# Eleven groups of three small products of ones between the first products of the dense part

## The chip, the cores and the metric

The kernel runs on all 8 cores of one Trainium2 chip, every core with the same program on one sequence of the batch of 8. A core has TensorE (PE; its weight loads are shown apart, as PEld), VectorE (DVE), ScalarE (ACT), GpSimd (POOL) and SyncE (SP), which meet by semaphores. The metric is the device time in microseconds of the slowest core, as the median of several runs.

## The reference

A decoder trunk of two layers on x of shape (8, 2048, 1024) in float32, with a conditioning vector c per sequence. Each layer has three parts, and each part is: RMSNorm, shift and scale from c, a function, a gate from c, and a residual add.

```python
for l in range(DEPTH):
    mod = c_act @ w_mod[l] + b_mod[l]
    ...
    h, gate = modulate(x, norm_g[l, 0], mod_f1)
    x = x + 0.5 * gate * swiglu(h, w_ffn_in[l, 0], w_ffn_out[l, 0])
    h, gate = modulate(x, norm_g[l, 1], mod_mx)
    ...
    x = x + gate * y
    h, gate = modulate(x, norm_g[l, 2], mod_f2)
    x = x + 0.5 * gate * swiglu(h, w_ffn_in[l, 1], w_ffn_out[l, 1])
return rmsnorm(x, final_g)
```

`swiglu` multiplies by two matrices of 1024 x 2816 and one of 2816 x 1024. The mixer `y` is a spatial gating and a short convolution between two projections in the first layer, and a causal pooling with small products in the second. Nearly all arithmetic lies in the matrix products. Those of the feed-forward parts and of the mixer's input are built in the kernel as seven block products in the place of eight, by sums of blocks of the weights and of the activations that DVE makes.

## The kernel before, in words

A core keeps its 2048 x 1024 residual stream in on-chip memory (X, four tiles of 512 tokens) and goes through ten phases: for each of five sub-layers (two feed-forward parts, the mixer, two feed-forward parts, with the pooling mixer worked in beside them) two passes of 1024 tokens. In a phase, weights come as pieces of 128 x 2048 floats by DMA from POOL's queue into six slots (SLOTS), normed activations stand in H, and products of 128 x 128 weights with 512 columns go into the eight PSUM banks (ps). ACT and DVE take them from there into ACTB, from which the second matrix is applied; DVE adds the result to X. `gu_segments` (line 1031) issues the first products of a feed-forward part and its inner `prod` four products into one bank. These products, with an index of `Sd.fill_to` (line 1723) or above, are called the dense part here.

Before the dense part stands a start of some 55 us: X and the first rows of the modulation weights arrive, ACT squares X, PE sums the squares by products with a block of ones (ONES, 128 x 128 in bf16), DVE and ACT build H. So that PE isn't idle, up to 150 (WARM, line 25) filler products of ones with squares (SQ) are put in, into bank 5:

```python
for n in range(WARM):
    op = add("pe", I("matmul", PS[5][:], ONES[:], SQ[:, n % NSQ, :], start=True, stop=True, skip_group_check=True),
             reads=[("SQ", n % NSQ), "ONES"], writes=[("ps", 5)], cost=0.0)
    op.issue, op.filler = c_pe(TT), 1
```

All instructions are entered into one list with what they read and write. `Sched.add` gives each a start time by a cost model, `Sched.relist` (line 178) goes through the list again and moves instructions of DVE, ACT and PE to where the model has them ready, most urgent first. It runs twice (line 1862). Fillers are taken only until the 21st product of the dense part has started (line 225). `Sched.emit` (line 281) then sorts by start time and writes out each engine's instructions in that order, with semaphore waits where another engine's work is needed:

```python
order = sorted((o for o in ops if o.filler < 2), key=lambda o: (o.start, o.idx))
...
for o in order:
    o.pos = len(by_eng[o.eng])
    by_eng[o.eng].append(o)
```

So a start time that is set after the last `relist` decides the place in an engine's queue, and nothing else. All instructions are issued by one helper, `I` (line 479), so the profile has all of them on line 480, and the names of what they write and read tell them apart: ps<-SQ,ONES are sums of squares and fillers, ps<-H,SLOTS and ps<-ACTB,SLOTS the dense part, ps<-ACTB the 128-column products of the spatial gating (`z_part`, line 1431).

Of the kernel before, what the change touches and what calls it, by code (L numbers as in the profile page):

```python
# [23 lines left out]
R_AT = 21  # L24
WARM = 150
PASSES = 2
SLG = (5, 6, 6, 7, 7, 7)


# [54 lines left out]
class Sched:  # L84
# [23 lines left out]
    def add(self, eng, fn, reads=(), writes=(), cost=0.1, dma=None, nbytes=0, after=0.0):  # L108

        ops = self.ops  # L110
        idx = len(ops)
        reads = list(reads)
        writes = list(writes)
        for k in list(reads):
            if isinstance(k, tuple) and k[0] == "ps":
                reads.remove(k)
                writes.append(k)
        deps = set()
        for k in reads:
            w = self.lastw.get(k)  # L120
            if w is not None:
                deps.add(w)
        for k in writes:
            w = self.lastw.get(k)
            if w is not None:
                deps.add(w)
            deps.update(self.readers.get(k, ()))
        choices = eng if isinstance(eng, list) else [(eng, fn, cost)]
        best = None
        for e, f, c in choices:  # L130
            ready = after
            for d in deps:
                o = ops[d]
                if o.eng == e and o.semkey is None and e == "pe":
                    t = o.end
                elif o.semkey is not None:
                    t = o.end
                else:
                    t = o.end + self.LAT[o.eng]
                if t > ready:  # L140
                    ready = t
            t = self.tl[e].find(ready, c)
            if best is None or t + c < best[0] - 1e-9:
                best = (t + c, t, e, f, c)
        _, t, e, f, c = best
        self.tl[e].put(t, c)
        op = Op()
        op.idx = idx
        op.eng = e
        op.fn = f  # L150
        op.deps = deps
        op.semkey = dma
        op.issue = c
        op.nbytes = nbytes
        op.bw = self.BW
        op.after = 0.0
        op.then = None
        op.gate = set()
        op.filler = 0
        op.start = t  # L160
        op.end = t + c
        if dma is not None:
            w = nbytes / self.BW
            s = self.wire.find(op.end + 1.5, w)
            self.wire.put(s, w)
            op.end = s + w + 2.0
        op.signal = False
        op.seq = 0
        op.dma_target = 0
        ops.append(op)  # L170
        for k in writes:
            self.lastw[k] = idx
            self.readers[k] = []
        for k in reads:
            self.readers.setdefault(k, []).append(idx)
        return op
# [302 lines left out]
def I(name, *a, **k):  # L479
    return lambda E: getattr(E, name)(*a, **k)  # L480
# [4 lines left out]
def build_nc():  # L485
# [37 lines left out]
    ONES = sb("ONES", [128, 128], BF16)  # L523
# [10 lines left out]
    PS = [nc.alloc_psum_tensor("ps%d" % b, [128, TT], F32) for b in range(8)]  # L534

    Sd = Sched()
    add = Sd.add
# [67 lines left out]
    def Xk(c, t):  # L605
        return ("X", c, t)
# [101 lines left out]
    def load_next(slot, after=()):  # L708
        if stream_at[0] >= len(stream):
            return  # L710
        pc = stream[stream_at[0]]
        stream_at[0] += 1
        pc.slot = slot
        pc.loaded = True
        if pc.kept is None:
            op = add("pool", I("dma_start", out=SL[:, slot, 0:pc.n], in_=pc.src, max_dma_last_dim=8192),
                     reads=list(after), writes=[("SL", slot, q) for q in range(7)], cost=0.7, dma=("SL", slot), nbytes=128 * 4 * pc.n)
        else:
            add("sp", I("dma_start", out=SL[:, slot, 1536:3584], in_=sums_d[pc.kept]), reads=[("SUMS", pc.kept)],
                writes=[("SL", slot, q) for q in range(3, 7)], cost=0.06, dma=("SS", slot), nbytes=128 * 4096)  # L720
            op = add("pool", I("dma_start", out=SL[:, slot, 0:1536], in_=pc.src[:, 0:1536], max_dma_last_dim=6144),
                     reads=list(after), writes=[("SL", slot, q) for q in range(3)], cost=0.7, dma=("SL", slot), nbytes=128 * 6144)
        pc.ready = op.end
# [951 lines left out]
    for t in range(2):  # L1675
        add("sp", I("dma_start", out=X[:, t, :, :], in_=xT[t].rearrange("p (c k) -> p c k", k=TT)),
            writes=[Xk(c, t) for c in range(NC)], cost=0.06, dma=("X", t), nbytes=128 * 16384)
# [15 lines left out]
# [3 lines that stand above are left out]
# [18 lines left out]
    fin["n", 0, 0] = True  # L1714
    for s, k in zip(range(NSLOT), SLG):
        load_next(s, [("MOD", 0, order0[k])])
# [3 lines left out]

    Sd.BW = Sched.BW

    Sd.fill_to = len(Sd.ops)


# [45 lines left out]
    for k, ph in enumerate(PHASES):  # L1771
# [6 lines left out]
        if sub[0] == "F":  # L1778
            l, i = sub[1], sub[2]
            s = 2 * i  # L1780
            for g in range(len(GROUPS)):
# [39 lines left out]
                if pm is not None:  # L1821
                    if pm == 0:
                        add("dve", I("memset", STAT[:, 0, 15:16], 0.0), reads=[("MOD", 0, q) for q in range(144)],
                            writes=["PMFREE", "CB"] + [("WM", x) for x in range(NWM)] + [("STG", x) for x in range(4)], cost=0.05)
# [36 lines left out]
    add("sp", None, reads=[("OUT", t, c) for t in range(4) for c in ((1, 3, 5, 7) if t < 3 else range(NC))], cost=0.01)  # L1861
    for _ in range(PASSES):
        Sd.relist(("dve", "act", "pe"))
    with nc.Block() as block:
        Sd.emit(nc, block)
    nc._sched = Sd
# [33 lines left out]
```

## Time and profile before

| | us |
|---|---|
| median of 3 runs | 1942.34 (1941.77 to 1942.77) |
| profiled execution, its own time | 1939.81 |
| its span, slowest core (core 0) | 1938.2 |
| spans of the other cores | 1906.8 to 1934.4 |
| PE busy in the span of core 0 | 1893.0 |
| DVE busy | 1719.3 |
| ACT busy | 1056.7 |
| POOL busy | 183.0 |

The span is the time from a core's first to its last instruction. Busy time of an engine is the time in which it had an instruction at work; products are pipelined, so one takes longer than the time from it to the next. The granted clock is the share of full speed (2.4 GHz) that the chip's throttle gave TensorE; 0.50 is the lower of its two levels, 1.2 GHz. A windows view has one row for a stretch: its length, then for PE, PEld, DVE, ACT and POOL the busy time and in brackets the number of instructions, then the mean granted clock, the share of the 16 DMA engines that was busy, and GB/s. In a row of instructions in order of time stand the start, the time from there to the end of the last one, the engine, the operation with what it writes and reads, the shape, and how many such instructions follow one another.

### The profile page before, as it was taken

How to read it: one execution, taken by the hardware profiler on the slowest of the kernel's cores; microseconds unless marked ns; L12 is line 12 of the kernel's file. 1: busy time of each engine (PE TensorE's matmuls, PEld its weight loads, DVE VectorE, ACT ScalarE, POOL GpSimd, SP SyncE). 2: the span in 40 equal slices, each digit the busy share in tenths (PEclk: the TensorE clock that was granted, in tenths of full speed). 3: DMA queues.
4: the chain of work that ended last, by engine and by line, in shares of the span. 5: the costliest groups of instructions: out<-in, count | busy, mean ns of one | idle time of the engine just before them, and what ended most of it. 6: DMA issues, size and time to landing. Idle time of an engine off the chain costs nothing.

```text
span 1938.2 us, 25442 instructions; the slowest of 8 cores (1906.8 to 1938.2 us)
## 1 busy us (share of the span) xinstructions
PE 1893.0 (98%) x8633; PEld 849.7 (44%) x8633; DVE 1719.3 (89%) x3326; ACT 1056.7 (55%) x1782; POOL 183.0 (9%) x349
## 2 busy tenths in 40 slices
PE   5999999999999999999999999999999999999997
PEld 2444444444444444444444444444444444444443
DVE  5886899989898999999999999998998899898865
ACT  4443755455757664565456545554556655574343
POOL 0000000000303000000000000000000000000000
PEclk6888899999999999999999999999999999999999
DMA  9867648755676668876877677745454545545852
GB/s 290 158 142 164 130 88 185 148 102 114 127 150 169 141 130 175 168 148 140 175 160 155 128 169 166 156 80 99 74 95 69 88 77 90 85 70 88 173 90 92
DMA packets 69390, 254.22 MB, mean 131 GB/s; under 512 B 7824, under 2 KB 7952, under 8 KB 69008
## 3 DMA queue, kind: packets, MB, share of 16 engines
q0 software_dynamic: 42192, 152.85, 47.4%
q1 hardware_dynamic: 26784, 98.96, 15.8%
q8 instruction: 73, 1.20, 0.2%
q10 hardware_dynamic: 288, 0.79, 0.1%
q14 instruction: 53, 0.43, 0.1%
HBM read 393.86 MB, written 11.53 MB: 209 GB/s over the span
## 4 chain that ended last, share of the span: by engine, by line
PE 93%; DMA 3%; ACT 2%; DVE 1%; SPq 0%; issue 0%; POOL 0%
PE ps L480 93%; DMA X<-xT 1%; DMA SLOTS<-win 1%; DMA WMOD<-wmod 1%; ACT SQ L480 1%; ACT TP L480 1%; DVE ACTB L480 0%; SPq L480 0%; ACT H L480 0%; ACT ps L480 0%; DVE X L480 0%; DVE TP L480 0%; DVE ps L480 0%; ACT L480 0%; ACT ACTB L480 0%
## 5 line engine op out<-in xcount | busy, mean ns | idle before, releaser
L480 PE MATMUL ps<-H,SLOTS 128*128 128x512 f16 x5376 | 1204.9, 384 | 8.1 <-ACT ps L480 3.4
L480 PEld LDWEIGHTS ps<-H,SLOTS 128*128 128x128 f16 x5376 | 527.7, 99 | 662.6 <-issue 90.0
L480 ACT ACTIVATE ps<-ps 128x512 f32<-128x512 f32 x716 | 416.3, 582 | 611.9 <-PE ps L480 601.5
L480 PE MATMUL ps<-ACTB,SLOTS 128*128 128x512 f16 x2780 | 623.1, 382 | 0.0
L480 PEld LDWEIGHTS ps<-ACTB,SLOTS 128*128 128x128 f16 x2780 | 273.9, 99 | 334.0 <-issue 26.4
L480 DVE TENSOR_TENSOR SLOTS<-SLOTS 128x512 f16<-128x512 f16 x1036 | 408.9, 417 | 10.6 <-DMA SLOTS<-win 6.1
L480 DVE SCALAR_TENSOR_TENSOR X<-ps,GH,X 128x512 f32<-128x512 f32 x424 | 307.8, 745 | 45.2 <-PE ps L480 38.6
L480 ACT ACTIVATE TP<-ps 128x512 f32<-128x512 f32 x408 | 241.6, 594 | 94.1 <-PE ps L480 89.7
L480 DVE TENSOR_TENSOR ACTB<-TP,ps 128x512 f16<-128x512 f32 x352 | 236.8, 682 | 34.4 <-PE ps L480 24.2
L480 POOL DMA_DIRECT2D SLOTS<-win x176 | 93.1, 530 | 1057.9 <-PE ps L480 993.1
L480 DVE TENSOR_TENSOR TP<-ps,TP 128x512 f32<-128x512 f32 x192 | 131.8, 687 | 55.6 <-ACT ps L480 54.4
L480 ACT ACTIVATE SQ<-X 128x512 bf16<-128x512 f32 x224 | 131.3, 623 | 85.1 <-DVE X L480 50.5
L480 DVE SCALAR_TENSOR_TENSOR WMOD<-WMOD,CB 128x1024 f32<-128x1024 f32 x130 | 157.8, 1216 | 3.0 <-DMA WMOD<-wmod 3.0
L480 DVE TENSOR_TENSOR ps<-ps,TP 128x512 f32<-128x512 f32 x192 | 133.4, 695 | 15.6 <-PE ps L480 12.4
L480 DVE TENSOR_TENSOR TP<-X,RS 128x512 f32<-128x512 f32 x192 | 127.8, 683 | 6.5 <-ACT ACTB L480 4.0
L480 DVE TENSOR_TENSOR ACTB<-ACTB 128x1024 f16<-128x1024 f16 (+1 forms) x188 | 103.9, 564 | 0.9
L480 ACT ACTIVATE H<-TP,MODT,AS 128x512 f16<-128x512 f32 x105 | 81.2, 806 | 31.9 <-DVE TP L480 31.6
L480 POOL DMA_DIRECT2D SLOTS<-wout x88 | 46.4, 528 | 496.8 <-PE ps L480 496.8
L480 PE MATMUL ps<-SQ,ONES 128*128 128x512 bf16 x173 | 58.1, 435 | 25.5 <-ACT SQ L480 23.4
L480 DVE TENSOR_TENSOR H<-H 128x1024 f16<-128x1024 f16 (+1 forms) x88 | 53.9, 634 | 1.7 <-ACT H L480 1.6
L480 ACT ACTIVATE PMH<-TP,MODT,AS 128x512 f16<-128x512 f32 x52 | 41.4, 806 | 11.8 <-DVE TP L480 11.6
L480 PEld LDWEIGHTS ps<-SQ,ONES 128*128 128x128 bf16 x173 | 18.3, 108 | 54.6 <-issue 41.2
(79 smaller groups left out, 548.5 us busy)
## 6 DMA issues: line engine op xcount, KB each, us to landing
SLOTS<-win POOLq DMA_DIRECT2D x176, 512.0 KB, 5.9
WMOD<-wmod SPq DMA_DIRECT2D x131, 512.0 KB, 5.3
SLOTS<-wout POOLq DMA_DIRECT2D x88, 512.0 KB, 5.4
SLOTS<-wab POOLq DMA_DIRECT2D x22, 512.0 KB, 6.4
outT<-X SPq DMA_DIRECT2D x14, 512.0 KB, 4.1
ACTB<-wmod SPq DMA_DIRECT2D x13, 512.0 KB, 24.9
X<-xT SPq DMA_DIRECT2D x2, 2048.0 KB, 20.7
X<-xT SPq DMA_DIRECT2D x8, 512.0 KB, 5.2
```

The lines of the kernel that those rows point to most:

```text
L480: return lambda E: getattr(E, name)(*a, **k)
```

## The change

Before the dense part is entered, 33 products are added to the list: ONES times ONES, 128 columns, into bank 7, in groups of three. After the last `relist` the products of the dense part are sorted by start time, and each group gets a start just behind that of the dense product whose number stands in SOFT, so that the groups stand behind the products 0, 1, 2, 4, 6, 8, 12, 15, 18, 22 and 27.

```diff
--- before.py
+++ after.py
@@ -24,6 +24,8 @@
 R_AT = 21
 WARM = 150
 PASSES = 2
+
+SOFT = (0, 1, 2, 4, 6, 8, 12, 15, 18, 22, 27)
 SLG = (5, 6, 6, 7, 7, 7)
 
 
@@ -1720,6 +1722,13 @@
 
     Sd.BW = Sched.BW
 
+    soft = []
+    for at in SOFT:
+        for n in range(3):
+            op = add("pe", I("matmul", PS[7][:, 0:128], ONES[:], ONES[:], start=True, stop=True, skip_group_check=True), reads=["ONES"],
+                     writes=[("ps", 7)], cost=0.0)
+            op.issue = 0.0
+            soft.append((at, op))
     Sd.fill_to = len(Sd.ops)
 
 
@@ -1861,6 +1870,9 @@
     add("sp", None, reads=[("OUT", t, c) for t in range(4) for c in ((1, 3, 5, 7) if t < 3 else range(NC))], cost=0.01)
     for _ in range(PASSES):
         Sd.relist(("dve", "act", "pe"))
+    dense = sorted((o for o in Sd.ops if o.eng == "pe" and o.idx >= Sd.fill_to), key=lambda o: o.start)
+    for n, (at, op) in enumerate(soft):
+        op.start = dense[at].start + 0.001 * (n + 1)
     with nc.Block() as block:
         Sd.emit(nc, block)
     nc._sched = Sd
```

PE's queue at the end of the start, before (H and SLOTS: activations and weights of the dense part; SQ, ONES: fillers):

```order
L480 MATMUL ps<-SQ,ONES 128x512 x19
L480 MATMUL ps<-H,SLOTS 128x512 x8
L480 MATMUL ps<-SQ,ONES 128x512 x2
L480 MATMUL ps<-H,SLOTS 128x512 x316
L480 MATMUL ps<-ACTB,SLOTS 128x512 x7
```

The dense part began there with 8 products in a row, 2 fillers, and 316 in a row.

The same place now, from the same fillers on:

```order
L482 MATMUL ps<-SQ,ONES 128x512 x19
L482 MATMUL ps<-H,SLOTS 128x512
L482 MATMUL ps<-ONES 128x128 x3
L482 MATMUL ps<-H,SLOTS 128x512
L482 MATMUL ps<-ONES 128x128 x3
L482 MATMUL ps<-H,SLOTS 128x512
```

Of the 8 products each of the first three is followed by a group of three.

And further down, where the last groups stand:

```order
L482 MATMUL ps<-H,SLOTS 128x512 x3
L482 MATMUL ps<-ONES 128x128 x3
L482 MATMUL ps<-H,SLOTS 128x512 x4
L482 MATMUL ps<-ONES 128x128 x3
L482 MATMUL ps<-H,SLOTS 128x512 x5
L482 MATMUL ps<-ONES 128x128 x3
L482 MATMUL ps<-H,SLOTS 128x512 x296
L482 MATMUL ps<-ACTB,SLOTS 128x512 x7
```

The last group stands behind the 28th product of the dense part; 296 products in a row follow it where 316 did.

On DVE, ACT, POOL and SP the order of instructions is the same as before.

## Rows read from the trace of the kernel before

**Rows 1.** Spans of all cores, us, with the mean granted clock.
```profile
core 0: 1938.2 us, clock 0.973
core 1: 1934.4 us, clock 0.979
...
core 3: 1907.0 us, clock 0.994
...
core 5: 1907.6 us, clock 0.988
core 6: 1911.1 us, clock 0.989
core 7: 1906.8 us, clock 0.994
```

**Rows 2.** The page, core 0: PE's busy time; shares of the chain.
```profile
PE 1893.0 (98%) x8633; PEld 849.7 (44%) x8633; DVE 1719.3 (89%) x3326; ACT 1056.7 (55%) x1782; POOL 183.0 (9%) x349
PE 93%; DMA 3%; ACT 2%; DVE 1%; SPq 0%; issue 0%; POOL 0%
```

**Rows 3.** Windows of core 0: length, busy us (count) by engine, clock, DMA.
```profile
core 0: us, PE busy (x) PEld busy (x) DVE busy (x) ACT busy (x) POOL busy (x), PEclk, DMA share, GB/s
54.00:58.00 4.00, 4.00 (x20) 1.86 (x19) 3.12 (x9) 2.47 (x5) 0.00 (x0) 1.00 1.01 220
60.00:62.00 2.00, 2.00 (x9) 0.75 (x8) 2.00 (x6) 1.67 (x4) 0.00 (x0) 0.87 1.06 168
62.00:219.00 157.00, 157.00 (x599) 64.87 (x598) 120.61 (x237) 66.36 (x114) 11.09 (x21) 0.81 0.71 155
219.00:221.00 2.00, 2.00 (x9) 0.84 (x8) 2.00 (x5) 1.60 (x4) 0.00 (x0) 0.88 0.65 129
221.00:300.00 79.00, 79.00 (x367) 35.82 (x366) 76.24 (x147) 52.96 (x94) 6.87 (x13) 1.00 0.52 94
300.00:1900.00 1600.00, 1591.03 (x7400) 718.65 (x7399) 1463.64 (x2806) 891.34 (x1507) 157.75 (x302) 1.00 0.63 126
```

**Rows 4.** Windows of core 1.
```profile
60.00:62.00 2.00, 2.00 (x10) 0.75 (x9) 1.92 (x6) 1.05 (x2) 0.00 (x0) 0.89 1.08 178
62.00:219.00 157.00, 157.00 (x600) 64.95 (x599) 120.76 (x235) 67.09 (x115) 11.07 (x21) 0.81 0.73 156
```

**Rows 5.** Windows of core 3, of the same die as core 0.
```profile
60.00:62.00 2.00, 1.97 (x10) 0.77 (x9) 2.00 (x6) 1.05 (x2) 0.00 (x0) 1.00 0.94 166
62.00:219.00 157.00, 156.90 (x727) 70.77 (x726) 143.70 (x287) 85.41 (x146) 13.73 (x26) 1.00 0.81 169
```

**Rows 6.** PE of core 0 in order of time, 48 to 76 us.
```profile
48.65 7.02 PE L480 MATMUL ps<-SQ,ONES 128*128 128x512 bf16 x19
55.51 1.89 PE L480 MATMUL ps<-H,SLOTS 128*128 128x512 f16 x8
57.24 0.59 PE L480 MATMUL ps<-SQ,ONES 128*128 128x512 bf16 x2
57.67 18.73 PE L480 MATMUL ps<-H,SLOTS 128*128 128x512 f16 x73
```

**Rows 7.** PE of core 2 in order of time, 590.5 to 591.5 us.
```profile
590.55 0.39 PE L480 MATMUL ps<-ACTB 128*128 128x128 f16 x4
590.78 0.38 PE L480 MATMUL ps<-H,SLOTS 128*128 128x512 f16 x1
590.99 0.39 PE L480 MATMUL ps<-ACTB 128*128 128x128 f16 x4
591.22 1.03 PE L480 MATMUL ps<-H,SLOTS 128*128 128x512 f16 x4
```

**Rows 8.** Groups of PE by form: busy us, mean ns of one, idle before.
```profile
L480 PE MATMUL ps<-ACTB 128*128 128x128 f16 x64 | 5.2, 219 | 0.9 <-ACT TP L480 0.8
```

## The prediction

> **What bounds the kernel now.** Start with the spans and granted clocks of all cores [rows 1]. Six cores end between 1906.8 and 1911.1 us; core 0 takes 1938.2 and core 1 takes 1934.4, with a mean granted clock of 0.973 and 0.979 where the six have 0.988 or more. The metric is the slowest core, so the time is core 0's, some 27 us behind the slowest core of the rest. All cores run the same program on equally large inputs, so the two differ in the clock and not in work.
>
> The page and the chain that ended last say what bounds a core: PE is busy for 98% of the span and makes 93% of the chain [rows 2]. Whatever slows a TensorE product, or is put between two of them, goes to the end nearly one to one.
>
> The windows of core 0 tell when its clock is low [rows 3]. From 54 to 58 us it is at 1.00, the upper of the two levels (2.4 GHz). Between 60 and 62 the mean is 0.87, from 62 to 219 it is 0.81, between 219 and 221 it is 0.88, and then 1.00 until 1900. So 0.81, a value between the levels 0.50 and 1.00, begins at 62 - 2 x 0.13 / 0.19 = 60.6 us and ends at 219 + 2 x 0.12 / 0.19 = 220.3 us: one stretch of about 160 us. On core 1 the same sum gives 60.8 for the start, and it has the same 0.81 stretch [rows 4]. Core 3, of the same die, has the same kind of work at those times and stays at 1.00 [rows 5].
>
> What PE did before the fall stands in its instructions in order of time [rows 6]. Until 55.51 us core 0 ran products on ones and squares. Then come 8 products on real data, 2 on ones, and from 57.67 an unbroken run of products on real data, each 512 columns at 2.4 GHz. The clock falls 5.1 us after the first of them and 2.9 us after the start of the run.
>
> Price of the stretch: between 62 and 219 us core 0 ran 599 products and core 3 ran 727 [rows 3, 5]. One at full clock takes 157 / 727 = 0.216 us, so core 0 lost 128 x 0.216 = 27.6 us there, and 27.6 x 159.7 / 157 = 28.1 us in the whole stretch. Without it core 0 would end at 1938.2 - 28.1 = 1910.1 and core 1 at 1906.3, which is where the other six end [rows 1]. So the stretch explains the whole gap, and nothing else of cores 0 and 1 needs explaining.
>
> **The change, part by part.** It adds 33 products, of 128 columns each, of a constant block of ones with itself, into bank 7, which no one reads in between. On DVE, ACT, POOL and SP nothing moves, no transfer is issued, and no product waits for anything new.
>
> Their price: near 590 us core 2 runs just such a mixture at clock 1.00 [rows 7]: 4 products of 128 columns from 590.55 to 590.78, one of 512 to 590.99, 4 again to 591.22. Four short ones take 0.23 us, or 0.0575 each, and the long one between them still takes its 0.21. 33 x 0.0575 = **1.9 us**, all on the path, since PE has no idle time there [rows 3]. Ends of that price: zero, if PE's delay fills waits that an undisturbed core has anyway; and 33 x 0.219 = 7.2 us, if each short product stood alone for the mean duration of its form [rows 8]. I take 1.9, because the rows of the mixture are the nearest.
>
> What it does to the density: before, all but 2 of the products of the first 5.1 us are on data: 5.1 - 2 x 0.216 = 4.7 us, or 92%. Now, counting along the new order (one product, three short ones, and so on, at 0.216 and 0.0575), 16 products on data fit into 5.1 us, so they fill 3.5 us, or 68%. The unbroken run begins after 28 x 0.216 + 33 x 0.0575 + 2 x 0.216 = 8.4 us, at 63.9 us, where it now begins at 57.67. The rise from little to full work is spread over 8.4 us.
>
> Does that keep the clock from falling? The rows before show no such ramp, so this is bounded from both sides: a gain of the whole 28.1 us on both cores, or none. What pulls towards the gain is that the level alone is not what brings the clock down. From 221 to 1900 us core 0 runs 7767 products at 1.00 and the clock never falls again [rows 3], and its sibling core 3 has run the same work at 1.00 in the same stretch [rows 5]. The fall came only after the one sudden start; the step back from 0.81 to 1.00 under full work brought none. Six of eight cores pass the same start without it, so the two cannot be far over the line. I take the gain.
>
> Here the Trainium skill (TensorE: Matmul & The Clock Gate, Part 1) speaks against the change: it tells of a peak-current limiter which takes a whole die to 13/16 of the clock once three cores of it run dense matmuls, and holds it while the load lasts. By that rule a softer start only delays the fall, and the time would stay, plus the 1.9 us. The value agrees with the rows (0.81); that the whole die falls and that it lasts with the load do not [rows 1, 3, 5]. The same section says that all-ones operands do not trip the limiter; no run here shows that yet.
>
> **Sum.** With both stretches gone the slowest core is core 6: 1911.1 + 1.9 = 1913.0 us. The profiled execution took 1939.81 us for a span of 1938.2, so 1.6 lie around it: 1914.6. The median of the runs, 1942.34, is 2.5 above that execution, so at the level of the median I forecast **1917.1 us**. Its own range is 1912 (no price for the short products and no offset to the median) to 1922 (7.2 us instead of 1.9). A measurement of this kernel can tell about 0.2%, here 3.9 us, from no change.
>
> **Rivals.**
> *The clock falls anyway.* Either full work on data, and not its sudden start, brings it down, so it falls a few us later; or a ramp of 8.4 us that has 68% density in its first 5.1 us is not soft enough; or only one of the two cores is spared, which leaves the maximum. For it: the fall is 5.1 us after the start, and the ramp is hardly longer; transfers are as dense as ever in those microseconds (DMA share 1.06 [rows 3]), and the change leaves those alone. Against it: 1679 us at full work and 1.00. It gives 1942.34 + 1.9 = 1944.2 us, no change that can be told. Chance 0.34.
> *The short products are dear, and the clock falls anyway.* Place: the 22 changes between forms on PE between 55 and 64 us. If a short product cannot hide its weight load behind its neighbour and each costs the 0.219 us of its form [rows 8], the start is 7.2 us longer and the stretch of 0.81 follows all the same: 1942.34 + 7.2 = 1949.5 us, slower by 0.37%. It decides from 3.9 / 33 = 0.118 us for each. Against it: twice 0.23 us for four in a mixture [rows 7]. Chance 0.07, with whatever else lengthens the start by over 3.9 us.
> *The change doesn't do what it says.* A scheduler places all other products, and could have gathered the short ones at one spot; but their start times are set after its last pass, and the order of PE now shows 11 groups between the products. No chance of its own.
>
> **How the numbers follow.** Faster 0.59 (1912 to 1922), within 0.2% 0.34 (about 1944), slower 0.07 (about 1949.5). The likeliest alone would leave out 0.41, so the range has to take in the second: 1912 to 1946, the upper end being 1944.2 and a little for the short products costing up to twice 1.9. Only the dear ones and the tails lie outside.
>
> **What would show it.** Right: no core has a stretch of 0.81, cores 0 and 1 end within 1907 to 1914 us like the others, and the 33 short products stand in the trace between 55 and 64 us in groups that take 0.17 us each at clock 1.00, with no wait on PE beside them. Wrong in the main point: 0.81 begins on core 0 or 1 some us later, or at the same time, and lasts some 160 us as before; then the spans of these two stay near 1936 to 1940. Wrong in the price: groups of over 0.35 us, or a stretch at 0.50 in the ramp.

## The result, and the profile after

The changed kernel took **1916.56 us** (median of 4 executions, 1915.24 to 1983.55) where the kernel before took 1942.50 (median of 4, 1941.77 to 1942.77); the ratio is 0.9863, with a 95% interval of 0.9834 to 0.9892. In one of the four the clock fell for long on four cores, which gave 1983.55; the ratio leaves it out.

The spans and clocks of all cores of the profiled execution, 1916.66 us by its own time, which answer to [rows 1]:

```profile
core 0: 1915.1 us, clock 0.995
core 1: 1912.5 us, clock 0.995
core 2: 1911.6 us, clock 0.995
core 3: 1909.4 us, clock 0.996
core 4: 1912.3 us, clock 0.995
core 5: 1908.6 us, clock 0.996
core 6: 1911.1 us, clock 0.994
core 7: 1908.0 us, clock 0.994
```

Cores 0 and 1 have joined the others: 0.995 where they had 0.973 and 0.979, and 23 and 22 us less. The windows of core 0, after (columns as in [rows 3]):

```profile
54.00:58.00 4.00, 4.00 (x28) 2.11 (x27) 3.06 (x9) 1.85 (x3) 0.00 (x0) 0.92 1.03 209
...
60.00:62.00 2.00, 2.00 (x17) 1.19 (x16) 2.00 (x7) 1.89 (x3) 0.00 (x0) 1.00 1.10 162
62.00:219.00 157.00, 155.51 (x724) 70.18 (x723) 141.65 (x282) 84.18 (x144) 13.26 (x25) 1.00 0.84 167
219.00:221.00 2.00, 2.00 (x11) 0.88 (x9) 2.00 (x6) 1.34 (x3) 0.00 (x0) 1.00 1.05 186
221.00:300.00 79.00, 78.73 (x366) 35.51 (x364) 76.24 (x149) 47.70 (x85) 6.89 (x13) 1.00 0.66 129
```

The row from 62 to 219 us has 724 products at 1.00 where [rows 3] had 599 at 0.81, and PE now waits there for 157 - 155.51 = 1.5 us. Undisturbed cores wait there too, by different amounts: core 3 waited 0.1 us in [rows 5], and core 6, in the same trace, 157 - 155.10 = 1.9. PE of core 0 in order of time, first and last groups:

```profile
55.78 0.38 PE L482 MATMUL ps<-H,SLOTS 128*128 128x512 f16 x1
56.00 0.33 PE L482 MATMUL ps<-ONES 128*128 128x128 bf16 x3
56.17 0.38 PE L482 MATMUL ps<-H,SLOTS 128*128 128x512 f16 x1
56.38 0.33 PE L482 MATMUL ps<-ONES 128*128 128x128 bf16 x3
56.55 0.38 PE L482 MATMUL ps<-H,SLOTS 128*128 128x512 f16 x1
...
63.94 0.33 PE L482 MATMUL ps<-ONES 128*128 128x128 bf16 x3
64.10 16.15 PE L482 MATMUL ps<-H,SLOTS 128*128 128x512 f16 x74
```

A group of three holds the next product on data back by 0.17 us (56.00 to 56.17), and the unbroken run begins at 64.10 us. In [rows 6] it began at 57.67.

So in this comparison the time came from where the prediction had it. What the comparison can't tell is whether the ramp is what kept the clock up. The kernel before is there with four executions that all fell, three of which are those that the time of the kernel before was taken from, and neither kernel's chip is on record; so the chip, or the hour, may have differed too. The experiments went to four chips, and told more than was asked.

### The profile page after: what moved, and what is told of

The parts are those of the page before. It is cut to its first block, busy times and chain, and to the rows that moved or that the text cites. A ratio compares the mean times of both kernels' runs of the same rounds, so it can differ in the third digit from the quotient of the medians.

```text
span 1915.1 us, 25508 instructions; the slowest of 8 cores (1908.0 to 1915.1 us)
## 1 busy us (share of the span) xinstructions
PE 1868.4 (98%) x8666; PEld 844.1 (44%) x8666; DVE 1715.5 (90%) x3326; ACT 1057.8 (55%) x1782; POOL 184.7 (10%) x349
## 4 chain that ended last, share of the span: by engine, by line
PE 86%; DMA 7%; DVE 3%; ACT 2%; issue 1%; POOL 0%; SPq 0%; POOLq 0%
PE ps L482 86%; DMA SLOTS<-win 3%; DMA WMOD<-wmod 1%; DMA X<-xT 1%; DVE ACTB L482 1%; DMA SLOTS<-wout 0%; DVE SLOTS L482 0%; ACT TP L482 0%; DVE X L482 0%; DVE TP L482 0%; DMA SLOTS<-wab 0%; ACT SQ L482 0%; DVE WMOD L482 0%; DVE ps L482 0%; POOL STAT L482 0%
## 5 line engine op out<-in xcount | busy, mean ns | idle before, releaser
L482 PE MATMUL ps<-H,SLOTS 128*128 128x512 f16 x5376 | 1186.8, 379 | 8.8 <-ACT ps L482 3.9
L482 PE MATMUL ps<-ACTB,SLOTS 128*128 128x512 f16 x2780 | 615.5, 379 | 0.5 <-DVE X L482 0.3
```

## Experiments

Each experiment ran with the kernel before beside it. An execution counts as one in which the clock fell when the spans of its cores lie more than 20 us apart; the others are called calm. Four groups of runs went to four chips, here A to D. In the first comparison (chip not known) all 4 executions of the kernel before fell, by their times and by the trace of a fifth, and 1 of 4 of the changed one.

Falls come in two sizes. One whose cores lie less than 40 us apart, so that one or two pairs of cores are some 30 us late as in the first comparison, is called a single stretch here. The others lie 45 to some 380 us apart and are called long. (On chip D all cores fell, so the size of the gap says nothing there.)

| kernel | chip | executions | clock fell in | of these, single stretches | median of the calm ones, us |
|---|---|---|---|---|---|
| before | A | 35 | 12 | 3 | 1916.45 |
| changed (e1_again) | A | 12 | 3 | 0 | 1917.91 |
| lump (e2_lump) | A | 14 | 3 | 0 | 1917.85 |
| data (e3_data) | A | 12 | 2 | 0 | 1917.82 |
| half (e4_half) | A | 12 | 3 | 2 | 1919.03 |
| before | B | 17 and 16 | 2 and 1 | 0 and 0 | 1914.39 and 1914.73 |
| long (e5_long) | B | 6 | 2 | 0 | 1927.87 |
| seven starts (e6_starts) | B | 5 | 1 | 0 | 1944.26 |
| cold (e7_cold) | B | 12 | 2 | 0 | 1913.15 |
| changed (e8_again) | B | 12 | 2 | 0 | 1916.18 |
| before | C | 23 | 13 | 8 | 1913.63 |
| changed (e9_again) | C | 12 | 2 | 1 | 1916.27 |
| cold (e10_cold) | C | 12 | 2 | 2 | 1913.22 |
| before | D | 11 | 11 | | none |
| lump (e11_lump) | D | 11 | 11 | | none |
| data (e12_data) | D | 8 | 8 | | none |

**The changed kernel again, chip A.** No edit.

> The changed kernel once more, beside the kernel before. Theory A (the sudden start of products on data brings the clock down on cores 0 and 1, and the ramp averts it): about 1916.5 us in nearly every run, no stretch of 0.81 on cores 0 and 1, the kernel before near 1942 in every run. Theory C (the fall comes by chance, whatever the kernel): both kernels mix runs near 1915 and runs near 1942, in like shares.

Measured: ratio 1.0004 (0.9994 to 1.0014), no difference. Here the kernel before is calm in 23 of 35 executions, and then it is as fast as the changed one. Theory A's "nearly every run" of the kernel before near 1942 did not come, and falls come to both kernels, so this speaks for theory C. It also gives the price of the ramp without its gain, 1917.91 - 1916.45 = 1.5 us between the calm medians, which the interval does not tell from nothing.

**All products of ones in one lump, chip A.**

```diff
-SOFT = (0, 1, 2, 4, 6, 8, 12, 15, 18, 22, 27)
+SOFT = (0,) * 11
```

> All 33 products of ones stand in one lump behind the first product of the dense part, so the dense part is as late as with the change (1.9 us) but starts as suddenly as before. Theory A: the stretch of 0.81 returns on cores 0 and 1 a few us after the start; 1942.5 + 1.9 = 1944.4 us. Theory B (the delay of 1.9 us, or products of ones close to the start, is what averts the fall): 1916.5 us with no stretch of 0.81.

Measured: 3 falls in 14, ratio 1.0006 (0.9996 to 1.0016). On a chip where the kernel before is mostly calm this tells neither A nor B apart.

**Data in place of ones, chip A.** The 33 results land in a bank that is overwritten before it is read, as with the ones.

```diff
-I("matmul", PS[7][:, 0:128], ONES[:], ONES[:], ...)
+I("matmul", PS[7][:, 0:128], SL[:, 0, n * 128:(n + 1) * 128], Hv4[:, n, 0:128], ...)
```

> The eleven groups stand where the change has them, but multiply weights and activations of the first piece in place of ones by ones (the results are not used). Theory A, in the form that products of ones draw little and so thin out the work on data: the fall returns, 1944.4 us. Theory D (it is the short form, with its changes of bank and length, that thins the work, whatever the data): 1916.5 us, no stretch of 0.81.

Measured: 2 falls in 12, ratio 1.0004 (0.9994 to 1.0013). Inconclusive for the same reason. The calm median is that of the ones to 0.1 us (1917.82 and 1917.91), so short products on data cost no more in all than those of ones.

**The first six groups alone, chip A.**

```diff
+SOFT = (0, 1, 2, 4, 6, 8)
```

> Only the first six groups (behind the products 0, 1, 2, 4, 6 and 8): 18 short products, 1.0 us, and the unbroken run begins some 2 us after the ninth product. Theory A, with the whole ramp needed: the stretch of 0.81 returns, 1943.5 us. If the first few products matter alone: 1915.7 us, 0.9 less than with eleven groups.

Measured: 3 falls in 12, two of them of one pair for one stretch (1944.54 and 1945.42 us, cores 6 and 7, and 0 and 1), ratio 1.0008 (0.9998 to 1.0018). No gain, and the expected 0.9 us less than with eleven groups did not show; differences of that size are within the interval.

**A ramp seven times as long, chip B.**

```diff
+SOFT = tuple(range(0, 20)) + tuple(range(20, 60, 2)) + tuple(range(60, 120, 3)) + tuple(range(120, 200, 4))
```

> A ramp of 80 groups in place of 11 (240 short products of ones, 13.8 us by the price of 0.0575 us each, spread over the first 200 products of the dense part, so that it takes some 57 us to full density). Theory A (the fall of the clock comes from the sudden start): executions with a stretch of 0.81, a third of those of the kernel before on the chip of the first experiments, all but vanish (0 or 1 of 12); undisturbed ones take 1918 + 13.8 = 1932 us. Theory C (the fall comes by chance and not from the start): a third of the executions has such stretches as before, the rest take 1932 us.

Measured: 2 falls in 6, calm ones at 1927.87, that is 13.5 us over the kernel before (13.8 were expected). The falls (2074 and 2104 us) are long ones, on all four cores of a die. A ramp of over 50 us does not prevent those.

**Six stops and new starts, chip B.** SOFT is (40, 80, 120, 160, 200, 240), each group 24 products of ONES with SQ, 512 columns.

> No ramp; six times in the first phase the dense part stops for 24 products of ones with squares (512 columns, 5.2 us) and starts again as suddenly as the first time. Cost without a fall: 144 x 0.216 = 31 us, 1949 us. Theory A: seven sudden starts in place of one, so falls in most executions (with a chance of a third for one start, over nine in ten for seven). Theory C: falls in a third of the executions, as before.

Measured: 1 fall in 5, calm ones at 1944.26, 29.9 us over the kernel before (31 expected). Seven sudden starts do not bring the clock down in most executions here. But on this chip one start goes with a fall in only 3 of 33 executions, not in the third that was expected; by that chance seven starts would give falls in about half (1 - (30/33)^7 = 0.49), from which 1 in 5 can't be told. What refutes theory A as a rule for every chip is the kernel before itself, which started suddenly and stayed calm in 30 of 33.

**No fillers ahead of the dense part, chip B.** The kernel before, with one number changed, which also changes the order that the scheduler finds on DVE and ACT.

```diff
-WARM = 150
+WARM = 21
```

> WARM is 21 in place of 150, without any ramp: the 19 filler products ahead of the dense part are gone, PE stands still for some 7 us before it, and the first products run at a granted clock of 0.50 until it rises. Cost without a fall: some 5 us by the half clock in the first 10 us, 1923 us. Theory A, if the step is from nothing to full work: falls in more than a third of the executions; if the rise of the clock splits the step in two: in fewer. Theory C: a third, as before.

Measured: 2 falls in 12, ratio 0.9991 (0.9982 to 1.0001): the low clock of the first products costs nothing that shows, where 5 us were expected. The trace of the second run of this kernel (e10_cold, chip C) has the likely reason. PE of core 0 in order of time, and its windows:

```profile
45.04 3.54 PE L480 MATMUL ps<-CT,WMOD 128*128 128x1 f32 x16 [0.75 <-DMA WMOD<-wmod]
50.11 0.58 PE L480 MATMUL ps<-SQ,ONES 128*128 128x512 bf16 x1 [1.53 <-DVE MODT L480]
51.03 1.86 PE L480 MATMUL ps<-H,SLOTS 128*128 128x512 f16 x4 [0.34 <-DMA SLOTS<-win]
53.37 12.95 PE L480 MATMUL ps<-H,SLOTS 128*128 128x512 f16 x53 [0.48 <-DVE SLOTS L480]
```

```profile
50.00:54.00 4.00, 3.07 (x7) 0.82 (x8) 4.00 (x12) 3.42 (x5) 1.59 (x3) 0.50 1.02 176
...
55.00:56.00 1.00, 1.00 (x4) 0.41 (x3) 1.00 (x4) 1.00 (x2) 0.00 (x0) 0.50 1.05 201
56.00:57.00 1.00, 1.00 (x6) 0.43 (x5) 0.78 (x3) 0.98 (x2) 0.00 (x0) 0.93 0.97 205
57.00:58.00 1.00, 1.00 (x7) 0.43 (x5) 0.49 (x1) 0.99 (x2) 0.00 (x0) 1.00 1.08 205
...
62.00:219.00 157.00, 155.81 (x721) 70.30 (x721) 143.37 (x287) 84.56 (x145) 13.73 (x26) 1.00 0.88 171
```

The first product on data starts at 51.03 us; in [rows 6] it waited behind the fillers until 55.51. It runs at 0.50 until 56 us. What the clock takes, the earlier start seems to give back; the changed order on DVE and ACT, which was not tested by itself, may have a part in it.

**The changed kernel, chip B.**

> The changed kernel a third time, on whichever chip this run gets. Theory C (falls by chance, in the same share with and without the ramp; the four executions of the kernel before near 1942 met such a time): a fifth to a third of the executions of both kernels have a stretch of 0.81, and between undisturbed ones the change costs 1.5 to 1.9 us (ratio 1.0008 to 1.0010). Theory E (one chip has a pair of cores that falls at every sudden start, and only there the ramp pays): if it is that chip, all executions of the kernel before near 1942 and those of the changed kernel near 1916.5; on any other chip as theory C.

Measured: 2 falls in 12 and 1 in 16 of the kernel before; ratio 1.0008 (0.9999 to 1.0017), 1916.18 - 1914.73 = 1.5 us. As theory C has it, though with fewer falls than its fifth to a third.

**The changed kernel and the cold one, chip C.**

> The changed kernel once more, for the share of executions in which the clock falls. Theory C: some 2 or 3 of 12, as for the kernel before beside it; between undisturbed ones the ratio is 1.0008 to 1.0010. Theory E, if this is the chip of the first comparison: the kernel before near 1942 in every execution, the changed one near 1916.5.

> The kernel without the 19 fillers ahead of the dense part and without a ramp, a second time, to see whether its 0.9991 against the kernel before holds. If the fillers ahead of the dense part buy nothing: 0.999 to 1.000, falls in some 2 or 3 of 12 by theory C. If that was chance, and the lower clock of the first products costs what it lasts: 1.002 or more.

Measured: the kernel before fell in 13 of 23 executions, 8 of them at 1938.80 to 1941.95 us with one or two pairs of cores some 25 to 30 us late, just as in the first comparison; the median of all its executions is 1939.04. The changed kernel fell in 2 of 12 (median of all 1916.73), the cold one in 2 of 12 (1913.62). The ratios, 0.9958 (0.9910 to 1.0006) and 0.9956 (0.9900 to 1.0012), take in calm executions and single stretches alike, and so lie between. If both kernels fell with one chance, a split as uneven as 13 of 23 and 2 of 12 would come about once in 38 times (Fisher's exact test, one-sided, 0.026); for the single stretches alone, 8 of 23 and 1 of 12, it is 0.09. And this is the one chip of three that favours the ramp: over chips A to C together the kernel before fell in 28 of 91 executions and the changed one in 7 of 36, and the same test gives 0.14. Theory A, or E in a weaker form, would have it so: on a chip where the start often brings one stretch, both kernels with a softer start meet it less. Theory E as it was put, all executions of the kernel before near 1942, did not come. The cold kernel has no ramp, but its products on data begin at half the clock, which may be another way to a softer start; nothing here tests that. Twelve executions each are few, and the lump, as late and as sudden, was not run on this chip.

**The lump and the data groups, chip D.**

> The lump of 33 products of ones behind the first product, a second time: as late as the change, as sudden as the kernel before. Theory F (two sorts of falls: one single stretch of some 160 us on a pair of cores at the start, which gives 1938 to 1947 us and which the ramp averts, and long falls of a whole die, which no version averts): on a chip where the kernel before meets single stretches in a third of its executions, as the lump's start is as sudden, so does the lump, 4 of 12. If the delay alone averts them: 0 or 1 of 12. On a chip where the kernel before hardly meets them, neither is told apart. Undisturbed executions: 1.5 us over the kernel before.

> The eleven groups with weights and activations in place of ones, a second time: the same places and lengths, no thinning of the work on data. Theory F in the form that ones draw little: single stretches as often as in the kernel before beside it (4 of 12 on a chip where it meets them in a third). If the changes of length and bank are what counts: 0 or 1 of 12, as for the change. Undisturbed executions: 1.5 us over the kernel before.

Measured: all executions of all kernels fell, the kernel before included (medians 2183.72 before, 2185.85 lump, 2186.91 data), so counts tell nothing. The traces do. The lump, core 0, windows and PE in order of time:

```profile
58.00:62.00 4.00, 4.00 (x20) 1.82 (x19) 1.43 (x5) 3.31 (x5) 0.00 (x0) 1.00 1.05 189
62.00:64.00 2.00, 2.00 (x10) 0.75 (x8) 2.00 (x5) 1.53 (x3) 0.00 (x0) 0.88 1.03 170
64.00:78.00 14.00, 14.00 (x55) 5.67 (x53) 11.86 (x26) 5.30 (x10) 1.06 (x2) 0.81 0.84 163
78.00:84.00 6.00, 6.00 (x29) 2.74 (x28) 4.66 (x10) 2.92 (x5) 0.53 (x1) 1.00 0.45 79
84.00:100.00 16.00, 16.00 (x64) 6.67 (x62) 13.68 (x27) 6.74 (x12) 1.06 (x2) 0.82 0.76 156
100.00:104.00 4.00, 4.00 (x20) 1.79 (x19) 3.70 (x7) 1.44 (x3) 0.53 (x1) 1.00 0.58 159
104.00:2100.00 1996.00, 1991.59 (x8013) 845.75 (x8034) 1636.37 (x3094) 985.99 (x1661) 170.48 (x325) 0.86 0.55 113
```

```profile
55.47 0.38 PE L482 MATMUL ps<-H,SLOTS 128*128 128x512 f16 x1
55.69 2.01 PE L482 MATMUL ps<-ONES 128*128 128x128 bf16 x33
57.53 1.67 PE L482 MATMUL ps<-H,SLOTS 128*128 128x512 f16 x7
59.04 0.59 PE L482 MATMUL ps<-SQ,ONES 128*128 128x512 bf16 x2
59.47 10.86 PE L482 MATMUL ps<-H,SLOTS 128*128 128x512 f16 x43
```

The clock falls in the row from 62 to 64 us (mean 0.88, so at 64 - 2 x 0.12 / 0.19 = 62.7), comes back before 78, falls again at about 84, is back at 100, and so on to the end: from 104 to 2100 us the mean is 0.86, a quarter of the time at 1.00. On this chip full work on data goes with a fall again and again, with no new start before it. And the first fall comes 5.2 us after the end of the lump (57.53), 7.2 after the first product on data. Now the groups with data, core 1, the later core of its pair (the short products have the names of the long ones here, so they are counted among the 23):

```profile
54.93 2.73 PE L482 MATMUL ps<-H,SLOTS 128*128 128x512 f16 x23
57.50 0.59 PE L482 MATMUL ps<-SQ,ONES 128*128 128x512 bf16 x2
57.93 12.48 PE L482 MATMUL ps<-H,SLOTS 128*128 128x512 f16 x62
```

```profile
54.00:58.00 4.00, 4.00 (x32) 2.28 (x30) 2.55 (x7) 1.64 (x4) 0.00 (x0) 1.00 1.05 209
58.00:60.00 2.00, 2.00 (x16) 1.05 (x15) 0.97 (x3) 1.98 (x3) 0.00 (x0) 1.00 1.02 180
60.00:62.00 2.00, 2.00 (x14) 1.08 (x13) 2.00 (x5) 1.48 (x3) 0.00 (x0) 0.81 1.12 168
```

Here 58 to 60 us is all at 1.00 and 60 to 62 at 0.81, so the clock falls at 60.0 us, 5.1 after the first product at 54.93. In the profile before it fell 5.1 us after 55.51 [rows 3, 6]. So in these traces the 33 products of ones put the fall off by about their own length, and short products on data in the same places did not. (The first 23 products of the data run hold 8 long and 15 short ones and take 57.50 - 54.93 = 2.57 us, so a short product on data costs (2.57 - 8 x 0.216) / 15 = 0.056 us, like one of ones.)

Two other pairs of chip D can be compared in the same way. The later core to start on data and the row of its fall, first in the lump run (cores 2 and 6), then in the data run (cores 2 and 7):

```profile
56.06 0.38 PE L482 MATMUL ps<-H,SLOTS 128*128 128x512 f16 x1
62.00:64.00 2.00, 2.00 (x10) 0.79 (x9) 2.00 (x5) 1.80 (x4) 0.00 (x0) 0.97 1.02 162
55.96 0.38 PE L482 MATMUL ps<-H,SLOTS 128*128 128x512 f16 x1
64.00:66.00 2.00, 2.00 (x10) 0.76 (x9) 1.92 (x6) 0.81 (x2) 0.00 (x0) 0.86 0.97 160
54.13 2.73 PE L482 MATMUL ps<-H,SLOTS 128*128 128x512 f16 x23
58.00:60.00 2.00, 2.00 (x15) 1.04 (x14) 1.77 (x6) 1.97 (x3) 0.00 (x0) 0.89 1.06 178
54.83 2.73 PE L482 MATMUL ps<-H,SLOTS 128*128 128x512 f16 x23
60.00:62.00 2.00, 2.00 (x15) 1.02 (x13) 2.00 (x5) 1.38 (x3) 0.00 (x0) 0.87 1.03 158
```

By the same sum the falls come 7.6 and 8.6 us after the first product on data with the lump, and 4.7 and 5.8 us after it with the groups of data: later by 2.9 and 2.8 us, where cores 0 and 1 have 2.1. So all three pairs agree in direction, each by one execution of each kernel. Counted from the end of the lump, as above, the first fall on the other pairs of chip D comes 4.7 to 6.5 us after the later core went to work on data; in the pair 4 and 5 of the data run the clock was down before that.

The Trainium skill (TensorE: Matmul & The Clock Gate, Part 1) says that all-ones operands do not trip the peak-current limiter; these two runs agree as far as they go, by the 2 to 3 us that the lump shifts the fall. It also says that a whole die goes to 13/16 and stays there while the load lasts. The value agrees (0.81). But in these traces the two cores of a pair fall within some 0.2 us of each other, each by its own time, and the pairs of a die apart (in the profile before cores 0 and 1 fell and core 3, of their die, did not [rows 4, 5]), and on cores 0 to 3 of chip D the clock comes back for some 5 us out of 20 under full load.

## Why the prediction was right

**The number** came out (1917.1 forecast, 1916.56 measured), and so did the steps that lead to it in this comparison: no 0.81 on cores 0 and 1, eleven groups in their places, 0.17 us for a group, the unbroken run at 64.1 us where 63.9 was forecast. That the gain came out is in part luck in the chip and the hour: the same two kernels later gave 1.0004 on chip A and 1.0008 on chip B.

**The price of the ramp**, 1.9 us, holds: 0.17 x 11 = 1.9 in the trace, 1.5 us between calm executions on chips A and B and 2.6 on chip C, with intervals wider than the differences between these. Part of it may go into waits that an undisturbed core has anyway, which the prediction had named as the lower end.

**The sum** hides two errors that cancel. The slowest core was to end at 1913.0 us and ended at 1915.1: core 0, not core 6. Its first product on data stands at 55.78 us, where that of core 6 stood at 54.67 in the kernel before, and that start was not in the sum. The stretch was worth 1938.2 + 1.9 - 1915.1 = 25.0 us and not 28.1; about half of the difference is the 1.5 us that core 0 waits between 62 and 219 us now that it is undisturbed, and the rest isn't explained. The 2.5 us between the profiled execution and the median, taken over from the kernel before, were not there either (1916.66 and 1916.56).

**The cause** was argued too widely. "The level alone is not what brings the clock down" was read from one execution on one chip, where the clock stayed up for 1679 us at full work. On chip D the clock falls over and over in an execution under full work, with no new start (though each fall after the first follows a step from 0.81 back to 1.00), and a ramp could only put off the first of them (so it is argued: the changed kernel was not run on that chip); on chips A and B falls come to all kernels in a minority of executions, with and without a ramp, and the run with seven starts had no more of them than can come from one. What is left of the forecast mechanism is this: a loss of the size of a single stretch on one or two pairs of cores happens in every execution of the kernel before in the first comparison and in a third of those on chip C (the one that was traced began 5.1 us after the first product on data), and there the changed kernel met it in 0 of 4 and 1 of 12. The counts favour the ramp; they don't show it, since the cold kernel without a ramp does as well on chip C (2 of 12), and on chip A the changed kernel was free of single stretches (0 of 12) where the kernel before had only 3 in 35.

**The rivals.** "The clock falls anyway" held its place: one of its grounds, that full work on data brings the clock down and not its sudden start, is what chip D speaks for. A rival was missing, and it holds most of the executions on chips A and B: that the stretch belongs to the chip and to chance, that a calm execution has nothing to avert, and that the change then costs 1.5 us, which a measurement of this kernel can't tell from no change. The short products were not dear, and the order of PE was as the listing had it.

What stays open: whether the chip of the first comparison has a pair that falls at each sudden start, which could not be met again; where in an execution the falls on chips A to C begin, since no trace holds one; and with that whether the ramp averts anything, which would take the kernel before, the lump and the changed one in turn on a chip like C, in many executions.

## What to carry to other kernels

Before a low clock is explained by the kernel, run the kernel before on more than one chip and count the executions in which the clock fell: here that share went from 3 in 33 to 11 in 11 for one and the same program, and was worth more than the edit. Products of ones are a cheap thing to put between products (0.056 us each at full clock, no instruction of another engine added), and 33 of them ahead of the work on data put a fall of the clock off by 2 to 3 us in the traces of chip D; but price these 33 as a loss of 1.5 to 2.6 us wherever the clock is up. Fillers that keep TensorE warm ahead of the real work can simply delay it: without them the first product on data came 4.5 us earlier on core 0, the calm executions were no slower than before, and some 3 us faster than those of the changed kernel on chips B and C.

## What the runs showed of the hardware that was not expected

The granted clock of 0.81 comes to pairs of cores (0 and 1, 2 and 3, 4 and 5, 6 and 7). In the profile before it held for 160 us once; on cores 0 to 3 of chip D, in the lump run, for some 15 us out of 20 throughout. And on cores 0 and 1 the time from the start of the work on data (on the later core of the two, and for the lump from its end) to the fall was 5.1, 5.2 and 5.1 us in three executions of three kernels, with no groups, a lump of ones before it, and groups of data in it; on the other pairs of chip D it was 4.7 to 6.5.
